# Compressed keys and values of a sparse-attention layer: bank reads shared with ScalarE, entries and key copies placed anew

## The chip, the cores and the metric

The kernel runs on one core of one Trainium2 chip. The metric is the device time of one execution in microseconds. The core's engines are TensorE (PE in the profile, its weight loads PEld), VectorE (DVE), ScalarE (ACT), GpSimd (POOL) and SyncE (SP, which issues the DMAs here). Each runs its own instructions in order, and they wait for each other by semaphores.

## The reference

A two-layer decoder trunk over 512 tokens of width 1024, in float32: layer 0 mixes by mLSTM and differential attention, layer 1 by sparse attention with three branches, and each has a SwiGLU network behind it. The change lies in layer 1's compressed branch. Its keys and values, four groups of 64 features, are cut into 31 blocks of 32 tokens at a distance of 16. A block is flattened and goes through a small network:

```python
def compress_blocks(kv, pos_emb, w1, w2):
    B, S, G, d = kv.shape
    r = CMP_BLOCK // CMP_STRIDE
    n_chunks = S // CMP_STRIDE
    n_cmp = n_chunks - r + 1
    ch = kv.reshape(B, n_chunks, CMP_STRIDE, G, d)
    blocks = jnp.concatenate([ch[:, j:j + n_cmp] for j in range(r)], axis=2)
    blocks = blocks + pos_emb[None, None, :, None, :]
    flat = blocks.transpose(0, 1, 3, 2, 4).reshape(B, n_cmp, G, CMP_BLOCK * d)
    return jax.nn.silu(flat @ w1) @ w2
```

The selected and the window branch have keys with a rotary embedding (KS and KW below); the queries (Q) are rotated as well.

## The kernel before

The weights come as **units**, some 512 KB each, in the order of `UNIT_LIST` (line 93). SP loads unit u into one of four buffers `raw`, once unit u-4 is split (`load`, line 550). Each float32 weight is split into a high part (`split_high`, ScalarE copies it into `w_high`, type fp32r; line 578) and a low part (`split_low`, VectorE subtracts; line 597), two buffers each. So the split of unit u+2 waits until TensorE is through with unit u. TensorE multiplies each tile three times, high by high, low by high and high by low (`mm3`, lines 705 to 707): 24 matmuls of 512 columns for a feature unit.

Layer 1 takes its units in this order: KC 0, KC 1, VC 0, VC 1 (keys and values to be compressed, two groups of 64 features each), KS 0, KS 1, KW 0, C1K 0, KW 1, Q 0, C1K 1, Q 1, C1K 2, Q 2, C1K 3, Q 3, Q 4, C1V 0, Q 5, C1V 1, Q 6, C1V 2, Q 7, GT, C1V 3, then VSW. C1K and C1V are the first weights of the small network. They have 12 matmuls of 256 columns, so the unit behind each of them comes soon, and its split is made in two **halves** (`HALVED`, line 98): the high half may start once TensorE is half through unit u-2 (semaphore `half_read`, ScalarE line 567), the second waits for its end (line 570); VectorE follows at lines 586 and 589.

On ScalarE and on VectorE one loop runs over the units: first the split of unit u+2, then `post(u)`, what is to be done with the result of unit u. Nothing is reordered: what waits in `post(u)` holds back the split of unit u+3.

- For a KC or VC unit VectorE **reads the bank** four times (line 1986), times `rinv`, the reciprocal norm of the tokens: each group of 64 features goes into `k_cmp_dup` or `v_cmp_dup` (`kvd`) twice, in the lower 64 partitions as it is, in the upper 64 moved by one token. The first of them waits for `rinv`, which ScalarE takes from TensorE in its `post(KC 0)` (line 1383).
- 32 **entries**, 16 of keys and 16 of values, are the inputs of C1K and C1V (four entries to a unit). For each, ScalarE adds the position and writes a high part (`cmp_high`, line 1553), and VectorE makes the low part (`cmp_low`, line 2055). `CMP_FIRST` (line 184) says at which unit's `post` which entries are made. TensorE waits for them (`hidden_unit`).
- For KS, KW and Q units VectorE takes the bank (line 1805), shuffles (line 1877) and does the rotary steps (lines 1887, 1888, 1892), with entries between them: the first behind the shuffle, the second behind line 1888, the rest at the end.
- ScalarE makes **key copies** (`duplicate_keys`, line 1532): four copies of 64 rows by 512 for each of KS 0, KS 1, KW 0 and KW 1, in the `post` of the unit that `DUP_AT` names, one place later. VectorE's next use but one of the same work buffer waits for them (`dup_done`).
- The hidden rows of the small network are turned on TensorE (line 1114), the keys' behind Q 3, the values' in VSW 0.

Of the kernel before, what the change touches and what calls it, by code (L numbers as in the profile page):

```python
# [5 lines left out]
ALU = mybir.AluOpType  # L6
# [5 lines left out]
P = 128  # L12
# [128 lines left out]
def plan_banks():  # L141
    bank, used, nxt, turn = {}, [0] * 8, 0, 0
    for kind, k in TILES:
# [22 lines left out]
        else:  # L166
# [14 lines left out]


DUP_AT = [("KS", 1), ("KW", 0), ("KW", 1), ("Q", 0)]
CMP_FIRST = {("VC", 1): 0, ("KS", 0): 1, ("KS", 1): 4, ("KW", 0): 7, ("KW", 1): 10, ("Q", 0): 13, ("Q", 1): 16,
             ("Q", 2): 19, ("Q", 3): 22, ("Q", 4): 25, ("Q", 5): 28, ("Q", 6): 30}


def cmp_entries(unit):
# [175 lines left out]
def trunk(nc, A, consts, out):  # L364
    with ExitStack() as ctx:
# [190 lines left out]

            return w[:, 0:KT * P].rearrange("p (k s g h) -> p k s g h", s=2, g=2, h=32)[:, :, side, :, 0:4]

        def split_high(act, u, it=0, per=0):
            if u >= UNITS:  # L560
                return
            w = width(u)
            act.wait_ge(S(f"raw_in{u % RAW}"), 16 * loads_in_slot(u) + it * (16 * per // RAW))
            if u in HALVED:

                act.wait_ge(S("half_read"), HALVED.index(u) + 1)
                act.activation(wh[u % SPL][:, 0:w // 2], raw[u % RAW][:, 0:w // 2], ACT.Copy)\
                    .then_inc(S("half_high"), 1)
                wait_unit(act, u - SPL)
                act.activation(wh[u % SPL][:, w // 2:w], raw[u % RAW][:, w // 2:w], ACT.Copy)\  # L570
                    .then_inc(S("split_high"), 1)
                return
            if u >= SPL:
                wait_unit(act, u - SPL, it, per)
            dst, src = wh[u % SPL][:, 0:w], raw[u % RAW][:, 0:w]
            if u == FIRST["IF"]:
                dst, src = if_columns(wh[u % SPL], 0), src.rearrange("p (k g h) -> p k g h", g=2, h=4)
            act.activation(dst, src, ACT.Copy).then_inc(S("split_high"), 1)  # L578
# [123 lines left out]
        def _(pe):  # L702
# [406 lines left out]
            def hidden_turn(name):  # L1109

                v = name == "C1V"
                pe.wait_ge(S("hidden_taken"), 1 + v)
                for hc in range(2):
                    mm = pe.transpose(aux[:, 3, hc * P:hc * P + CCOLS],
                                      hrow[0:CCOLS, 256 * v + hc * P:256 * v + (hc + 1) * P], ident[0:CCOLS, 0:CCOLS])
                mm.then_inc(S("hidden_turned"), 1)

            for m in range(2):
# [250 lines left out]
        def _(act):  # L1369
# [70 lines left out]
            def post(u):  # L1440
# [17 lines left out]
                elif name == "VM" and j == 1:  # L1458
                    act.wait_ge(S("lam_sums"), 2)
                    act.activation(lame, lams, ACT.Exp).then_inc(S("lam_exps"), 1)  # L1460
                elif name == "VM" and j == 2:
                    act.wait_ge(S("u_col"), 1)
                    act.activation(em2col, aux[:, 0, 16:32], ACT.Exp, scale=2.0).then_inc(S("exp_negm"), 1)
                    for h in range(3):
                        act.wait_ge(S("negM_rows"), h + 1)
                        act.activation(nmb[:, tcol(h)], aux[:, 1 + h, :], ACT.Copy).then_inc(S("negM_taken"), 1)
                elif name in ("WO0", "WO1"):
                    n = 1 + 2 * int(name[2])
                    wait_taken(act, (name, j))
                    norm_y(n, j)  # L1470
                    if j == 7:
                        split_high(act, u + SPL)
                    square(n, j)
                elif name == "KC" and j == 0:
                    norm_rows(2)
                elif name in ("Q", "KS", "KW", "VC"):
                    if (name, j) == ("Q", 3):
                        act.wait_ge(S("hidden_turned"), 1)
                        act.activation(hid.rearrange("p (k g n) -> p k g n", k=2, n=CPAD)[:, :, :, 0:NCMP],
                                       aux[:, 3, 0:256].rearrange("p (k m) -> p k m", m=P)[:, :, 0:CCOLS]  # L1480
                                       .rearrange("p k (g n) -> p k g n", n=NCMP), ACT.Copy).then_inc(S("hidden_in"), 1)
                    if (name, j) == ("Q", 4):
                        act.wait_ge(S("kc_product"), 1)
                        kc_pairs = kcd.rearrange("p (g n) -> p g n", n=2 * CPAD)
                        for a in range(2):
                            half, other = slice(64 * a, 64 * a + 64), slice(64 - 64 * a, 128 - 64 * a)
                            act.activation(kc_pairs[other, :, col(a, CPAD)],
                                           kc[other, 0:P].rearrange("p (g n) -> p g n", n=CPAD), ACT.Copy, scale=0.0)
                            o = act.activation(kc_pairs[half, :, col(a, CPAD)],
                                               ps(("KCD", 0))[half, 0:P].rearrange("p (g n) -> p g n", n=CPAD), ACT.Copy)  # L1490
                        o.then_inc(bank_free(("KCD", 0)), 1)
                    for e in cmp_entries((name, j)):
                        cmp_high(e)
                    if (name, j) in DUP_AT:
                        duplicate_keys(DUP_AT.index((name, j)))
                elif name in ("C1K", "C1V") and j == 3:
                    wait_unit(act, u)
                    act.activation(hrow[0:CCOLS, col(name == "C1V", 256)], aux[0:CCOLS, 2, 0:256], ACT.Silu)\
                       .then_inc(S("hidden_taken"), 1)
                    if name == "C1V":  # L1500
                        cmp_exp(1)
                elif name == "GT":
                    cmp_exp(0)
                elif name == "VSW":
                    if j == 0:

                        act.wait_ge(S("hidden_turned"), 2)
                        act.wait_ge(S("v_hidden_zero"), 2)
                        for hc in range(2):
                            turned = aux[:, 3, hc * P:hc * P + CCOLS].rearrange("p (g n) -> p g n", n=NCMP)  # L1510
                            act.activation(vhid[hc].rearrange("p (g h n) -> p g h n", h=4, n=CPAD)[:, :, :, 0:NCMP],
                                           turned.unsqueeze(2).to_broadcast([P, GROUPS, 4, NCMP]), ACT.Copy)\
                               .then_inc(S("hidden_in"), 1)
                    if j == 1:
                        act.wait_ge(S("gates_added"), 1)
                        act.activation(gates, gates, ACT.Sigmoid).then_inc(S("gates"), 1)
                    if j == 3:
                        for i in (0, 2):
                            act.wait_ge(S("rows_done"), i + 1)
                            taken_scaled(vsw[:, tcol(i)], (name, i), i)  # L1520
                    cmp_take(j)
                    if j < 2:
                        cmp_exp(j + 2)

            def duplicate_keys(k):

                r = 8 + k
                act.wait_ge(S("rope_done"), 3 * r + 3)
                dst = ksd if k < 2 else kwd
                for g in range(2):  # L1530
                    for half in range(2):
                        o = act.activation(dst[64 * half:64 * half + 64, tcol(2 * (k % 2) + g)],
                                           tmp[r % 2][64 * g:64 * g + 64, 0:T], ACT.Copy)
                o.then_inc(S("dup_done"), 1)

            def cmp_exp(i):
                act.wait_ge(S("c_shifted"), i + 1)
# [8 lines left out]
            def cmp_high(e):  # L1546
                v, c = e // CHUNKS, e % CHUNKS
                if c == 0:
                    wait_taken(act, (("KC", "VC")[v], 0))
                    wait_taken(act, (("KC", "VC")[v], 1))  # L1550
                if v and c % 4 == 0:
                    wait_unit(act, AT["C1K", c // 4])
                act.activation(kph[:, c * CCOLS:(c + 1) * CCOLS].rearrange("p (g n) -> p g n", n=NCMP),
# [153 lines left out]
            ffn(0)  # L1707
            for u in range(FIRST["KC"], FIRST["WO1"]):
                if u < FIRST["WO1"] - 1:
                    split_high(act, u + SPL)  # L1710
                post(u)

            def rows_high(q):
# [63 lines left out]
        def _(dve):  # L1777
# [128 lines left out]
            def post(u):  # L1906
# [68 lines left out]
                elif name in ("KC", "VC"):  # L1975
# [4 lines left out]
                        dve.wait_ge(S("rinv"), 3)  # L1980
                    dst = kvd[name == "VC"]

                    for g in range(2):
                        rows_ = slice(64 * g, 64 * g + 64)
                        for half in range(2):
                            o = dve.tensor_tensor(dst[64 * half:64 * half + 64,
                                                      (2 * j + g) * T:(2 * j + g + 1) * T - half],
                                                  ps((name, j))[rows_, half:T], rinv[rows_, half:T], ALU.mult)
                    o.then_inc(bank_free((name, j)), 1)
                    for e in cmp_entries((name, j)):  # L1990
                        cmp_low(e)
                elif name == "GT":
# [649 lines left out]
```

## Time and profile before

| | us |
|---|---|
| median of 3 runs | 1340.31 (1339.85 to 1340.4) |
| the profiled execution | 1340.15 |
| its span, first to last instruction | 1338.4 |
| TensorE busy | 1319.6 |
| VectorE busy | 698.0 |
| ScalarE busy | 553.1 |

The profile is of one execution. Its page gives the busy time of each engine, the groups of instructions by line, and the chain that ended last, of which TensorE has 89% and VectorE 5%. The mean granted clock of TensorE is 0.999 of its full speed. In the timelines a row is one instruction or a few alike; a wait is put down to the instruction that released it. The matmuls of TensorE overlap in the records (0.39 us each, one every 0.23 us), so their distance from start to start counts.

### The profile page before, as it was taken

The numbers are of one execution on the slowest core, as the hardware profiler recorded it, in microseconds if no ns is written. First come the engines' busy times: TensorE is split into PE (matmuls) and PEld (weight loads), VectorE is DVE, ScalarE is ACT, GpSimd is POOL, SyncE is SP. The second block draws the span as 40 slices with busy tenths as digits, with TensorE's granted clock in tenths as the row PEclk, the third lists the DMA queues.
The fourth block names the chain that finished last, engine by engine and source line by source line (L and its number), as shares of the span: only waits on it lengthen the run. The fifth ranks groups of instructions, "written<-read, shape, count | busy, mean of one in ns | idle before, by whom it ended". The sixth has DMA issues, their size and how long they took to land.

```text
span 1338.4 us, 17983 instructions
## 1 busy us (share of the span) xinstructions
PE 1319.6 (99%) x6420; PEld 1050.8 (79%) x6420; DVE 698.0 (52%) x1282; ACT 553.1 (41%) x1012; POOL 229.8 (17%) x233
## 2 busy tenths in 40 slices
PE   9999999999999999999999999999999999999997
PEld 7677688888888888888878865567888888888887
DVE  5479886544333334332699778775533344332222
ACT  4435665443333332222274457784433333332222
POOL 2047571221111110100000002112211111110100
PEclk9999999999999999999999999999999999999999
DMA  8331222333333333332244310000333333343311
GB/s 239 89 79 49 63 64 66 92 94 95 94 98 103 95 106 108 107 87 78 80 118 124 96 32 1 17 2 17 106 97 96 94 94 94 95 119 106 104 47 64
DMA packets 205481, 114.12 MB, mean 85 GB/s; under 512 B 5712, under 2 KB 202576, under 8 KB 205296
## 3 DMA queue, kind: packets, MB, share of 16 engines
q1 hardware_dynamic: 204800, 112.97, 29.1%
q0 software_dynamic: 416, 0.35, 0.3%
q8 instruction: 33, 0.54, 0.2%
q14 instruction: 24, 0.20, 0.0%
q10 hardware_dynamic: 208, 0.06, 0.0%
HBM read 111.27 MB, written 2.10 MB: 85 GB/s over the span
## 4 chain that ended last, share of the span: by engine, by line
PE 89%; DVE 5%; ACT 2%; issue 2%; POOL 1%; DMA 0%; POOLq 0%; DVEq 0%; SPq 0%; ACTq 0%
PE acc L705 24%; PE acc L707 24%; PE acc L706 24%; PE acc L1285 3%; PE aux L1272 2%; PE aux L1190 2%; PE acc L1190 1%; DVE w_low L597 1%; PE acc L1272 1%; ACT w_high L578 1%; PE acc L1172 1%; PE aux L1151 1%; PE aux L883 0%; PE acc L825 0%; PE aux L893 0%
## 5 line engine op out<-in xcount | busy, mean ns | idle before, releaser
L597 DVE TENSOR_TENSOR w_low<-raw,w_high 128x1024 fp32r<-128x1024 f32 (+2 forms) x185 | 247.5, 1338 | 491.9 <-ACT w_high L578 491.7
L705 PE MATMUL acc<-y_high,w_high 128*128 128x512 f32 x992 | 392.0, 395 | 2.5 <-DVE w_low L589 2.0
L707 PE MATMUL acc<-y_high,w_low 128*128 128x512 f32 x992 | 386.6, 390 | 0.0
L706 PE MATMUL acc<-y_low,w_high 128*128 128x512 f32 x992 | 386.2, 389 | 0.0
L578 ACT ACTIVATE w_high<-raw 128x1024 fp32r<-128x1024 f32 (+2 forms) x186 | 205.7, 1106 | 301.4 <-PE acc L707 296.1
L705 PEld LDWEIGHTS acc<-y_high,w_high 128*128 128x128 f32 x992 | 185.8, 187 | 43.1 <-DVE w_low L589 3.3
L707 PEld LDWEIGHTS acc<-y_high,w_low 128*128 128x128 f32 x992 | 185.7, 187 | 40.0
L706 PEld LDWEIGHTS acc<-y_low,w_high 128*128 128x128 f32 x992 | 185.9, 187 | 38.7 <-issue 0.7
L705 PE MATMUL acc<-ffn_high,w_high 128*128 128x512 f32 (+1 forms) x374 | 141.0, 377 | 0.0
L706 PE MATMUL acc<-ffn_low,w_high 128*128 128x512 f32 (+1 forms) x374 | 140.8, 377 | 0.0
L707 PE MATMUL acc<-ffn_high,w_low 128*128 128x512 f32 (+1 forms) x374 | 140.8, 377 | 0.0
L2513 POOL TENSOR_TENSOR work<-work,work 128x512 f32<-128x512 f32 x44 | 56.9, 1294 | 417.7 <-DVE work L1805 417.7
L1567 ACT ACTIVATE ffn_high<-work 128x512 f32 (+1 forms) x44 | 27.8, 632 | 148.4 <-POOL work L2513 148.4
L1805 DVE TENSOR_TENSOR work<-acc,rinv 128x512 f32<-128x512 f32 x107 | 73.2, 684 | 17.1 <-PE acc L707 9.7
L2499 POOL TENSOR_TENSOR work<-work,work 128x512 f32<-128x512 f32 x31 | 42.1, 1359 | 224.0 <-ACT work L1379 223.5
L705 PEld LDWEIGHTS acc<-ffn_high,w_high 128*128 128x128 f32 x374 | 70.4, 188 | 12.9
L706 PEld LDWEIGHTS acc<-ffn_low,w_high 128*128 128x128 f32 x374 | 70.4, 188 | 12.9
L707 PEld LDWEIGHTS acc<-ffn_high,w_low 128*128 128x128 f32 x374 | 70.4, 188 | 12.8
L1732 ACT ACTIVATE score<-score,neg_max 128x384 f32<-128x384 f32 (+3 forms) x128 | 68.6, 540 | 14.1 <-DVE neg_max L2378 14.1
L2605 POOL TENSOR_TENSOR o_rows<-o_rows,work 128x512 f32<-128x512 f32 x16 | 20.4, 1273 | 249.7 <-DVE work L2400 249.7
L1562 ACT ACTIVATE work<-work 128x512 f32<-128x512 f32 x44 | 27.8, 632 | 80.3 <-DVE work L1805 80.3
L1372 ACT ACTIVATE y_high<-residual,feature_params 128x512 fp32r<-128x512 f32 x32 | 22.8, 722 | 51.5 <-DVE residual L2005 33.0
(342 smaller groups left out, 1685.8 us busy)
## 6 DMA issues: line engine op xcount, KB each, us to landing
raw<-in_l_w_in_dram SPq DMA_DIRECT2D x44, 512.0 KB, 3.8
raw<-in_l_w_gate_dram SPq DMA_DIRECT2D x44, 512.0 KB, 3.8
raw<-in_l_w_up_dram SPq DMA_DIRECT2D x44, 512.0 KB, 3.8
raw<-in_l_w_down_dram SPq DMA_DIRECT2D x32, 704.0 KB, 4.5
raw<-in_l_w_out_dram SPq DMA_DIRECT2D x16, 512.0 KB, 3.5
x_rows<-in_x_dram SPq DMA_DIRECT2D x4, 512.0 KB, 7.6
raw<-in_l_cmp_w_k_dram SPq DMA_DIRECT2D x4, 512.0 KB, 3.7
raw<-in_l_cmp_w_v_dram SPq DMA_DIRECT2D x4, 512.0 KB, 3.7
```

The costliest lines, as they stand in the source:

```text
L578: act.activation(dst, src, ACT.Copy).then_inc(S("split_high"), 1)
L597: dve.tensor_tensor(dst, src, high.bitcast(F32), ALU.subtract).then_inc(S("split_low"), 1)
L705: pe.matmul(o, ah, bh, start=first, stop=False)
L706: pe.matmul(o, ah, bl, start=False, stop=False)
L707: return pe.matmul(o, al, bh, start=False, stop=last)
L1190: pe.matmul(scores_at(n), qrot[a, q], k, start=True, stop=True).then_inc(S("s_scores"), 1)
L1272: mm = pe.transpose(turn_bank(("probs", t))[:, c + s * P:c + (s + 1) * P], probs[:, col(s)], ident)
L1285: mm = pe.matmul(ps(("OB", b))[64 * g:64 * g + 64, :].rearrange("p (h q) -> p h q", q=P), vsw[:, v:v + HD], probs[:, 4 * g:4 * g + 4, col(s)],
L1732: act.activation(probs_at(n), probs_at(n), ACT.Exp, scale=-1.0, bias=nmx[:, n % 16:n % 16 + 1], accum_out=rsum[:, n % 16:n % 16 + 1]).then ...
L1805: return dve.tensor_tensor(dst, ps(tile)[lo:hi, cols], rinv[lo:hi, cols], ALU.mult)
L2499: pool.tensor_tensor(tmp[0][:, 0:T], tmp[0][:, 0:T], tmp[1 + m % 2][:, 0:T], ALU.add)\
L2513: pool.tensor_tensor(up, tmp[2 * (t % 2)][:, 0:T], up, ALU.mult).then_inc(S("ffn_prod"), 1)
```

## The change

Four edits, all in layer 1's compressed branch and the keys beside it.

1. For a KC or VC unit VectorE reads the bank twice instead of four times, plus one column: the even group into the lower partitions, the odd group, moved by one token, into the upper ones. ScalarE makes the other halves from these (`move_tokens`, two copies of 64 rows by 511) in its `post` of the same unit, behind VectorE's reads. `cmp_high` waits for these copies (`tokens_moved`) instead of the reads.
2. Entries: three at VC 0, three at VC 1, one at KS 0, one at KS 1, two at KW 0, one at KW 1, then three a unit from Q 0 to Q 6. Before: one at VC 1, then three a unit, with two at Q 5 and Q 6.
3. Of the key copies of KS 0 and KW 0 the first two stay where they were; the third goes between the two high halves of the split of KW 1 and Q 1, the fourth behind the second half.
4. The hidden rows are activated and turned with 128 rows instead of 124.

```diff
--- before.py
+++ after.py
@@ -181,8 +181,9 @@
 
 
 DUP_AT = [("KS", 1), ("KW", 0), ("KW", 1), ("Q", 0)]
-CMP_FIRST = {("VC", 1): 0, ("KS", 0): 1, ("KS", 1): 4, ("KW", 0): 7, ("KW", 1): 10, ("Q", 0): 13, ("Q", 1): 16,
-             ("Q", 2): 19, ("Q", 3): 22, ("Q", 4): 25, ("Q", 5): 28, ("Q", 6): 30}
+COPIES_LATE = {("KW", 1): 0, ("Q", 1): 2}
+CMP_FIRST = {("VC", 0): 0, ("VC", 1): 3, ("KS", 0): 6, ("KS", 1): 7, ("KW", 0): 8, ("KW", 1): 10, ("Q", 0): 11,
+             ("Q", 1): 14, ("Q", 2): 17, ("Q", 3): 20, ("Q", 4): 23, ("Q", 5): 26, ("Q", 6): 29}
 
 
 def cmp_entries(unit):
@@ -556,7 +557,7 @@
 
             return w[:, 0:KT * P].rearrange("p (k s g h) -> p k s g h", s=2, g=2, h=32)[:, :, side, :, 0:4]
 
-        def split_high(act, u, it=0, per=0):
+        def split_high(act, u, it=0, per=0, after_half=None):
             if u >= UNITS:
                 return
             w = width(u)
@@ -566,6 +567,8 @@
                 act.wait_ge(S("half_read"), HALVED.index(u) + 1)
                 act.activation(wh[u % SPL][:, 0:w // 2], raw[u % RAW][:, 0:w // 2], ACT.Copy)\
                     .then_inc(S("half_high"), 1)
+                if after_half:
+                    after_half()
                 wait_unit(act, u - SPL)
                 act.activation(wh[u % SPL][:, w // 2:w], raw[u % RAW][:, w // 2:w], ACT.Copy)\
                     .then_inc(S("split_high"), 1)
@@ -1111,8 +1114,7 @@
                 v = name == "C1V"
                 pe.wait_ge(S("hidden_taken"), 1 + v)
                 for hc in range(2):
-                    mm = pe.transpose(aux[:, 3, hc * P:hc * P + CCOLS],
-                                      hrow[0:CCOLS, 256 * v + hc * P:256 * v + (hc + 1) * P], ident[0:CCOLS, 0:CCOLS])
+                    mm = pe.transpose(aux[:, 3, col(hc)], hrow[:, 256 * v + hc * P:256 * v + (hc + 1) * P], ident)
                 mm.then_inc(S("hidden_turned"), 1)
 
             for m in range(2):
@@ -1471,9 +1473,11 @@
                     if j == 7:
                         split_high(act, u + SPL)
                     square(n, j)
-                elif name == "KC" and j == 0:
-                    norm_rows(2)
-                elif name in ("Q", "KS", "KW", "VC"):
+                elif name in ("Q", "KS", "KW", "KC", "VC"):
+                    if (name, j) == ("KC", 0):
+                        norm_rows(2)
+                    if name in ("KC", "VC"):
+                        move_tokens(name, j)
                     if (name, j) == ("Q", 3):
                         act.wait_ge(S("hidden_turned"), 1)
                         act.activation(hid.rearrange("p (k g n) -> p k g n", k=2, n=CPAD)[:, :, :, 0:NCMP],
@@ -1495,7 +1499,7 @@
                         duplicate_keys(DUP_AT.index((name, j)))
                 elif name in ("C1K", "C1V") and j == 3:
                     wait_unit(act, u)
-                    act.activation(hrow[0:CCOLS, col(name == "C1V", 256)], aux[0:CCOLS, 2, 0:256], ACT.Silu)\
+                    act.activation(hrow[:, col(name == "C1V", 256)], aux[:, 2, 0:256], ACT.Silu)\
                        .then_inc(S("hidden_taken"), 1)
                     if name == "C1V":
                         cmp_exp(1)
@@ -1522,16 +1526,30 @@
                     if j < 2:
                         cmp_exp(j + 2)
 
+            def move_tokens(name, j):
+
+                dst = kvd[name == "VC"]
+                first, second = 2 * j * T, (2 * j + 1) * T
+                wait_taken(act, (name, j))
+                act.activation(dst[64:128, first:first + T - 1], dst[0:64, first + 1:first + T], ACT.Copy)\
+                   .then_inc(S("tokens_moved"), 1)
+                act.activation(dst[0:64, second + 1:second + T], dst[64:128, second:second + T - 1], ACT.Copy)\
+                   .then_inc(S("tokens_moved"), 1)
+
+            def duplicate_part(k, part):
+
+                r, g, half = 8 + k, part // 2, part % 2
+                if part == 0:
+                    act.wait_ge(S("rope_done"), 3 * r + 3)
+                o = act.activation((ksd if k < 2 else kwd)[64 * half:64 * half + 64, tcol(2 * (k % 2) + g)],
+                                   tmp[r % 2][64 * g:64 * g + 64, 0:T], ACT.Copy)
+                if part == 3:
+                    o.then_inc(S("dup_done"), 1)
+
             def duplicate_keys(k):
 
-                r = 8 + k
-                act.wait_ge(S("rope_done"), 3 * r + 3)
-                dst = ksd if k < 2 else kwd
-                for g in range(2):
-                    for half in range(2):
-                        o = act.activation(dst[64 * half:64 * half + 64, tcol(2 * (k % 2) + g)],
-                                           tmp[r % 2][64 * g:64 * g + 64, 0:T], ACT.Copy)
-                o.then_inc(S("dup_done"), 1)
+                for part in range(2 if k in COPIES_LATE.values() else 4):
+                    duplicate_part(k, part)
 
             def cmp_exp(i):
                 act.wait_ge(S("c_shifted"), i + 1)
@@ -1546,8 +1564,7 @@
             def cmp_high(e):
                 v, c = e // CHUNKS, e % CHUNKS
                 if c == 0:
-                    wait_taken(act, (("KC", "VC")[v], 0))
-                    wait_taken(act, (("KC", "VC")[v], 1))
+                    act.wait_ge(S("tokens_moved"), 4 + 4 * v)
                 if v and c % 4 == 0:
                     wait_unit(act, AT["C1K", c // 4])
                 act.activation(kph[:, c * CCOLS:(c + 1) * CCOLS].rearrange("p (g n) -> p g n", n=NCMP),
@@ -1707,7 +1724,10 @@
             ffn(0)
             for u in range(FIRST["KC"], FIRST["WO1"]):
                 if u < FIRST["WO1"] - 1:
-                    split_high(act, u + SPL)
+                    late = COPIES_LATE.get(stage_of(u + SPL))
+                    split_high(act, u + SPL, after_half=None if late is None else lambda k=late: duplicate_part(k, 2))
+                    if late is not None:
+                        duplicate_part(late, 3)
                 post(u)
 
             def rows_high(q):
@@ -1980,13 +2000,12 @@
                         dve.wait_ge(S("rinv"), 3)
                     dst = kvd[name == "VC"]
 
-                    for g in range(2):
-                        rows_ = slice(64 * g, 64 * g + 64)
-                        for half in range(2):
-                            o = dve.tensor_tensor(dst[64 * half:64 * half + 64,
-                                                      (2 * j + g) * T:(2 * j + g + 1) * T - half],
-                                                  ps((name, j))[rows_, half:T], rinv[rows_, half:T], ALU.mult)
-                    o.then_inc(bank_free((name, j)), 1)
+                    first, second = 2 * j * T, (2 * j + 1) * T
+                    low, high = slice(0, 64), slice(64, 128)
+                    dve.tensor_tensor(dst[low, first:first + T], ps((name, j))[low, :], rinv[low, :], ALU.mult)
+                    dve.tensor_tensor(dst[low, second:second + 1], ps((name, j))[high, 0:1], rinv[high, 0:1], ALU.mult)
+                    dve.tensor_tensor(dst[high, second:second + T - 1], ps((name, j))[high, 1:T], rinv[high, 1:T],
+                                      ALU.mult).then_inc(bank_free((name, j)), 1)
                     for e in cmp_entries((name, j)):
                         cmp_low(e)
                 elif name == "GT":
```

## Rows read from the trace of the kernel before

**Rows 1.** The page, part 1: busy us, share of the span, instructions.
```profile
PE 1319.6 (99%) x6420; PEld 1050.8 (79%) x6420; DVE 698.0 (52%) x1282; ACT 553.1 (41%) x1012; POOL 229.8 (17%) x233
```

**Rows 2.** Waits of TensorE, 640 to 800 us: total, times, longest.
```profile
PE acc L705 <- DVE w_low L589: 2.0, 2, 1.0
```

**Rows 3.** Timeline of TensorE: start us, us, instruction, idle before and releaser.
```profile
655.08 0.39 PE L705 MATMUL acc<-y_high,w_high 128*128 128x512 f32 x1
...
660.52 0.39 PE L705 MATMUL acc<-y_high,w_high 128*128 128x512 f32 x1
...
679.41 0.50 PE L705 MATMUL acc<-y_high,w_high 128*128 128x512 f32 x1 [1.00 <-DVE w_low L589]
...
684.98 0.39 PE L705 MATMUL acc<-y_high,w_high 128*128 128x512 f32 x1
...
693.00 0.50 PE L705 MATMUL acc<-y_high,w_high 128*128 128x512 f32 x1 [0.99 <-DVE w_low L589]
...
713.71 0.50 PE L705 MATMUL acc<-y_high,w_high 128*128 128x512 f32 x1 [0.38 <-DVE w_low L597]
```

**Rows 4.** Timeline of ScalarE, 640 to 742 us.
```profile
650.28 1.05 ACT L578 ACTIVATE w_high<-raw 128x1024 fp32r<-128x1024 f32 x1
...
677.04 0.63 ACT L570 ACTIVATE w_high<-raw 128x512 fp32r<-128x512 f32 x1
677.58 1.30 ACT L1553 ACTIVATE cmp_in_high<-k_cmp_dup,feature_params 128x124 fp32r<-128x124 f32 x3
678.78 2.54 ACT L1532 ACTIVATE k_sel_dup<-work 64x512 f32<-64x512 f32 x4
```

**Rows 5.** Timeline of VectorE, 640 to 755 us.
```profile
650.42 2.79 DVE L1986 TENSOR_TENSOR k_cmp_dup<-acc,rinv 64x512 f32<-64x512 f32 x4 [4.07 <-ACT rinv L1383]
653.25 1.23 DVE L597 TENSOR_TENSOR w_low<-raw,w_high 128x1024 fp32r<-128x1024 f32 x1
654.50 2.79 DVE L1986 TENSOR_TENSOR k_cmp_dup<-acc,rinv 64x512 f32<-64x512 f32 x4
...
668.57 0.69 DVE L1805 TENSOR_TENSOR work<-acc,rinv 128x512 f32<-128x512 f32 x1
...
670.25 0.69 DVE L1887 TENSOR_TENSOR work<-work,shape_constants 128x512 f32<-128x512 f32 x1
670.85 0.69 DVE L1888 TENSOR_TENSOR work<-work,shape_constants 128x512 f32<-128x512 f32 x1
...
672.75 1.22 DVE L597 TENSOR_TENSOR w_low<-raw,w_high 128x1024 fp32r<-128x1024 f32 x1
673.90 0.68 DVE L1805 TENSOR_TENSOR work<-acc,rinv 128x512 f32<-128x512 f32 x1
...
678.08 0.67 DVE L586 TENSOR_TENSOR w_low<-raw,w_high 128x512 fp32r<-128x512 f32 x1
678.68 0.68 DVE L589 TENSOR_TENSOR w_low<-raw,w_high 128x512 fp32r<-128x512 f32 x1
...
742.37 1.23 DVE L597 TENSOR_TENSOR w_low<-raw,w_high 128x1024 fp32r<-128x1024 f32 x1 [2.69 <-ACT w_high L578]
743.51 0.68 DVE L1805 TENSOR_TENSOR q_raw<-acc,rinv 128x512 f32<-128x512 f32 x1
...
745.01 0.69 DVE L1887 TENSOR_TENSOR work<-q_raw,shape_constants 128x512 f32<-128x512 f32 x1
...
746.34 0.69 DVE L1892 TENSOR_TENSOR q_rot<-work,work 128x512 f32<-128x512 f32 x1
```

**Rows 6.** Groups of VectorE by form: count, busy us, mean ns, idle before.
```profile
L2378 DVE DVE_READ_ACCUMULATOR2_ANT neg_max<- 128x1 f32 x128 | 10.6, 83 | 0.0
...
L1794 DVE TENSOR_SCALAR msq<-aux 128x4 f32<-128x4 f32 x3 | 0.5, 155 | 0.0
```

**Rows 7.** Groups of TensorE by line, same columns.
```profile
L1114 PE MATMUL aux<-shape_constants,hidden_rows 124*128 124x124 f32 x4 | 0.8, 282 | 0.0
```

## The prediction

> **What bounds the kernel now.** I read the page's busy shares first: TensorE is busy for 99% of the span, the next engine, VectorE, for 52% [rows 1]. So only what makes TensorE wait, or gives it other work, can move the end. The waits of TensorE come next, cut to the stretch of the compressed keys and values (640 to 800 us): two waits of 1.0 us for the second low half of a weight split on VectorE [rows 2]. TensorE's timeline places them in front of KW 1 (679.41) and Q 1 (693.00), shows one of 0.38 us in front of Q 4 (713.71), and gives the beat: 5.44 us from one unit to the next, 5.57 us behind a unit that began late [rows 3]. A stall that is taken away anywhere is gained whole, and one that is added is paid whole, since nothing later waits.
>
> Who is late there? Read ScalarE's and VectorE's timelines side by side. In front of KW 1 ScalarE's second half of the split starts at 677.04, as soon as KW 0 is multiplied, and ends at 677.67 [rows 4]; VectorE, busy with the rotary steps of KS 1 and its entries, starts the first low half at 678.08 and the second at 678.68, which ends at 679.36 [rows 5]. So at both waits of 1.0 us VectorE's queue is the last, not ScalarE's. With VectorE free, KW 1 could start about 0.9 us sooner (677.67 + 0.03 + 0.68 + 0.05 = 678.43).
>
> **Part 1, half of the bank reads become ScalarE copies.** Now a KC or VC unit costs VectorE four reads, 2.79 us, 0.70 apart [rows 5]. After the change: a read of 64 rows by 512 (0.70), one column, a read of 64 by 511 (0.69). No row shows a read of one column. The nearest is the bank read of 128 by 4 at 0.155 us; from below there is the accumulator read of 0.083 [rows 6], from above a whole read of 0.69, which gets little weight, as the durations of VectorE go by columns (0.155 for 4, 0.69 for 512, 1.23 for 1024). I take 0.16, so a T (the reads of one unit) is 1.55 us. ScalarE gets a move M of two copies of 64 by 511: four key copies of 64 by 512 take 2.54 us [rows 4], so M = 1.27 us. Does VectorE's saving count? Only if nothing new waits, and M is a wait: it is queued in front of the next ScalarE split.
>
> The order on ScalarE is: split of unit u+2 (SH, 1.06), then M of unit u, which waits for T of unit u, then entries; on VectorE: low split of u+2 (SL, 1.23, which waits for SH), then T of unit u, 1.25 behind SL's start [rows 5]. Before the change nothing of ScalarE waited for T in this stretch, and SH of VC 1 ran at 650.28, ahead of the reads. Now the two engines form one ring. Handovers are 0.03 (ScalarE to VectorE), 0.04 (VectorE to ScalarE) and 0.05 us (VectorE to TensorE), from ends and starts in the timelines [rows 3 to 5]. I walk it from the first read, 650.42, which waits for rinv as before:
>
> T of KC 0 ends 651.97; M 652.01 to 653.28; SH of VC 1 to 654.34; SL 654.37 to 655.60. TensorE wanted VC 1 at 655.08 [rows 3] and gets it at 655.65: 0.57 late.
> T of KC 1 655.62 to 657.17; M to 658.48; SH of KS 0 to 659.54; SL 659.57 to 660.80. KS 0 is wanted at 655.65 + 5.57 = 661.22: in time.
> T of VC 0 to 662.37; M to 663.68; the three entries that now sit here, 0.40 each (three in 1.30, the next instruction 1.20 behind the first [rows 4]), to 664.89; SH of KS 1 to 665.95; SL 665.98 to 667.21. Wanted at 666.66, there at 667.26: 0.60 late.
> T of VC 1 from 667.23 to 668.78; M to 670.09; three entries to 671.30; SH of KW 0 to 672.36; SL 672.39 to 673.62; KW 0 starts 673.67, wanted at 667.26 + 5.57 = 672.83: 0.84 late.
>
> The ring takes 5.20 us a unit without entries, less than TensorE's 5.44, and 6.41 with three: it holds for VC 0 and VC 1, where the change puts entries.
>
> The Trainium skill, VectorE: DVE Perf Modes, section "Two Vector instructions with no wait between them", says that a Vector instruction whose input or output starts in another group of 32 partitions than the last one's waits until that has finished. The bank reads stand 0.70 apart and two rotary steps on all rows 0.60 (670.25 and 670.85) [rows 5], so the rows agree, and the three new reads, which change halves as well, keep the 0.70. Had they run unheld, the four T would be 0.1 to 0.2 shorter each and the sum below 0.4 to 0.8 us less.
>
> **Part 2, entries sooner.** KS 0, KS 1 and KW 1 keep one entry of three, KW 0 two of three. On VectorE the block behind a take lasts 4.18 us with three entries (668.57 to 672.75) and 4.18 again (673.90 to 678.08) [rows 5]. Q 7 has none: 743.51 to its last add at 746.34, plus 0.60, is 3.43 [rows 5]; an entry behind the shuffle fills a wait there and is estimated at 0.18 (take to first rotary step 1.68 at KS 0, 1.50 at Q 7). So a block with one entry is 3.61, 0.57 less (bounds 0.56 and 0.70, the second if no wait is laid bare).
> VectorE's block for KS 0 now starts at 672.39 + 1.25 = 673.64 instead of 668.57: 5.07 later. From there to KW 1's second low half VectorE never waits for ScalarE (its first and second halves are there by 678.6 and 680.2). Two blocks save 2 x 0.57. KW 1 starts at 679.41 + 5.07 - 1.14 = 683.34, **3.93 us late**. Between KW 1 and Q 1 TensorE sets the pace again: the split of C1K 1 waits for the end of KW 1, so that the block of KW 1 begins 3.93 late too and is 0.57 shorter. Q 1 starts 3.36 late, and its old wait of 1.0 us has become some 0.4.
> KW 0 with two entries (about 3.82) ends before the split of Q 0 is wanted: VectorE through with it at 688.26, TensorE wants it at 688.91. Cover: 0.65 us.
>
> **Part 3, key copies around the halves.** Four copies stay four copies; one goes between the halves of the split and one behind. ScalarE's second half was already in time [rows 4], so taking the copies from in front buys nothing. The third copy lies in ScalarE's wait for TensorE, the fourth (0.64) delays the next entries, which have over 1 us to spare, and the read of KW 0, which waits for the copies: those end 0.64 us behind the second half, while VectorE then still works on the low half (0.68). Nothing; at worst 0.1 us each at KW 1 and at C1K 2. Without that cover it is 0.64.
>
> **Part 4, turns of 128 rows.** Two transposes for the keys and two for the values, 282 ns each at 124 rows [rows 7], now 128 by 128. Q 4 behind the first pair waits for VectorE [rows 3]; the second pair ends up to 0.02 us later. Nothing. The activations go by columns, also unchanged. Behind Q 1 the entries stay three a unit up to Q 6 (one more at Q 5 and at Q 6, 0.35 us of VectorE each, under its waits for ScalarE; the one behind Q 6 is 2.69 us [rows 5]). Loads are issued behind the low split of the unit four places ahead and land in some 4 us by the page: covered. The wait in front of Q 4 stays.
>
> **Sum.** 5.07 - 1.14 - 0.57 = +3.36 us on the profiled execution's 1340.15 us: 1343.5. The median of the runs shown is 1340.31, 0.16 above it; I forecast **1343.6**.
>
> **Rivals.**
> *The reads are cheaper than I set them.* The column costs 0.08 and the reads follow at 0.60: T = 1.37, four of them save 0.72: +2.6 us, 1342.9. For it: no row has these reads in this order. Against: the old reads, which change halves as well, are all 0.70 apart. Chance 0.17.
> *The ring never closes (the other side, not slower).* Place: ScalarE's queue between rinv and the split of KW 0. If T, M, three entries, SH and SL together took under 5.44 us instead of 6.41, TensorE would stay ahead, and only the shorter blocks would count: 0.57 at KW 1 and 0.57 at Q 1, -1.1 us, 1339.1. It decides from 1.0 us less a unit, as would copies of 0.15 us; the four copies of this shape take 0.63 each [rows 4]. Chance 0.07. Even all three waits gone would be -2.4 us plus restarts, so a gain of over 0.2% is nearly excluded.
> *The clock.* The wait in front of KW 1 grows from 1.0 to 2.7 us. Through today's waits the granted clock stays 1.00; no row shows a longer one here. If the lower level (1.2 of 2.4 GHz) held for one unit behind it, 5.4 us more: 1349. Chance 0.03.
> The Trainium skill, TensorE: Matmul & The Clock Gate, Part 1, says that idleness lowers the clock; no run here shows whether this wait does.
> *The cuts do nothing and the ring is longer* (a column read costs a full 0.69, or the copies wait on each other): 4 x 0.5 more, +5.5 us, 1345.8. Chance 0.08.
>
> **How the numbers follow.** Forecast (+3.0 to +3.9) 0.65, the rivals as above. 0.2% of 1340 is 2.7 us, about what a measurement of this kernel can tell from no change. The forecast's own band lies over it, the first rival just around it. Slower by over 0.2%: 0.65 x 0.95 + 0.17 x 0.4 + 0.03 + 0.08 = 0.79, lowered to 0.72 for what I may have overlooked in the queues; same 0.25; faster 0.03. The range goes from 1341.8 (below the first rival, with 0.8 for errors of many small terms) to 1345.3.
>
> **What the profile after would show.** VC 1, KS 1 and KW 0 each start behind a wait of 0.5 to 0.9 us for a VectorE low split whose releaser is ScalarE; ScalarE idles for VectorE's reads before each move; the wait in front of KW 1 is 2.5 to 2.8 us, that of Q 1 about 0.4, that of Q 4 as now. VectorE is less busy and waits more. I am wrong if SH of VC 1 starts before 652.5, if KW 0 starts on the beat, or if KW 1 waits under 1 us.

## The result, and the profile after

The changed kernel takes 1345.29 us (median of 9 runs, 1343.67 to 1345.57) against 1340.03 (9 runs): 1.0035 of before, 95% interval 1.0026 to 1.0043. The forecast was 1343.6, with 1341.8 to 1345.3. The nine runs lie in two groups, three at 1343.67 to 1344.02 and six at 1345.20 to 1345.57; what parts them is the subject of one experiment (busy wait). The median lies 0.01 us inside the forecast's upper end, three of the nine runs lie above it.

The page says little: TensorE is 1.7 us busier and its span 5.2 us longer than in [rows 1], 1343.6 us.

```profile
PE 1321.3 (98%) x6420; PEld 1050.8 (78%) x6420; DVE 693.5 (52%) x1278; ACT 558.1 (42%) x1020; POOL 229.7 (17%) x233
```

The waits of TensorE from 640 to 800 us, total, times and longest. In the changed kernel the matmuls of a unit stand in lines 708 to 710, the low splits in 600 (whole), 589 and 592 (halves). These answer to [rows 2].

```profile
PE acc L708 <- DVE w_low L592: 3.0, 2, 2.5
PE acc L708 <- DVE w_low L600: 2.1, 4, 0.7
```

Where before there were two waits of 1.0 us for a second half, there is one of 2.5 us and one of 0.4, and four for a whole split (three of them new). TensorE's timeline has them all (start, duration, instruction, idle before), as [rows 3] had them of before:

```profile
655.34 0.50 PE L708 MATMUL acc<-y_high,w_high 128*128 128x512 f32 x1 [0.46 <-DVE w_low L600]
...
667.05 0.50 PE L708 MATMUL acc<-y_high,w_high 128*128 128x512 f32 x1 [0.52 <-DVE w_low L600]
...
673.52 0.50 PE L708 MATMUL acc<-y_high,w_high 128*128 128x512 f32 x1 [0.71 <-DVE w_low L600]
...
683.21 0.50 PE L708 MATMUL acc<-y_high,w_high 128*128 128x512 f32 x1 [2.55 <-DVE w_low L592]
...
684.50 0.56 PE L710 MATMUL acc<-y_high,w_low 128*128 128x512 f32 x1
...
685.28 0.63 PE L709 MATMUL acc<-y_low,w_high 128*128 128x512 f32 x1
685.70 0.63 PE L710 MATMUL acc<-y_high,w_low 128*128 128x512 f32 x1
...
688.13 0.39 PE L710 MATMUL acc<-y_high,w_low 128*128 128x512 f32 x1
...
697.89 0.50 PE L708 MATMUL acc<-y_high,w_high 128*128 128x512 f32 x1 [0.43 <-DVE w_low L592]
...
718.61 0.50 PE L708 MATMUL acc<-y_high,w_high 128*128 128x512 f32 x1 [0.36 <-DVE w_low L600]
```

In order: VC 1, KS 1, KW 0, KW 1 (683.21, behind 2.55 us), four matmuls inside KW 1, Q 1 and Q 4. ScalarE's timeline shows what the new waits are made of. Lines 1534 and 1536 are the moves, 581 a split, 1570 the entries; compare with [rows 4], where the split of VC 1 ran at 650.28, right behind `rinv`.

```profile
649.43 0.60 ACT L1385 ACTIVATE rinv<-aux 128x512 f32<-128x512 f32 x1 [6.60 <-PE aux L799]
651.66 0.63 ACT L1534 ACTIVATE k_cmp_dup<-k_cmp_dup 64x511 f32<-64x511 f32 x1 [1.63 <-DVE k_cmp_dup L2007]
652.31 0.63 ACT L1536 ACTIVATE k_cmp_dup<-k_cmp_dup 64x511 f32<-64x511 f32 x1
652.97 1.06 ACT L581 ACTIVATE w_high<-raw 128x1024 fp32r<-128x1024 f32 x1
656.91 0.63 ACT L1534 ACTIVATE k_cmp_dup<-k_cmp_dup 64x511 f32<-64x511 f32 x1 [2.88 <-DVE k_cmp_dup L2007]
...
662.17 0.63 ACT L1534 ACTIVATE v_cmp_dup<-v_cmp_dup 64x511 f32<-64x511 f32 x1 [2.89 <-DVE v_cmp_dup L2007]
...
663.48 1.31 ACT L1570 ACTIVATE cmp_in_high<-k_cmp_dup,feature_params 128x124 fp32r<-128x124 f32 x3
664.70 1.04 ACT L581 ACTIVATE w_high<-raw 128x1024 fp32r<-128x1024 f32 x1
...
679.18 0.63 ACT L1544 ACTIVATE k_sel_dup<-work 64x512 f32<-64x512 f32 x1
679.83 0.63 ACT L573 ACTIVATE w_high<-raw 128x512 fp32r<-128x512 f32 x1
```

The move at 651.66 idled 1.63 us for VectorE's reads, and the split of VC 1 had to stand behind it until 652.97. It is the same again at 656.91 and 662.17, with 2.9 us of idling each, and for VC 1 at 668.63. On VectorE (the three reads are lines 2005 to 2007, the take of KS 0 is at 673.50; compare [rows 5]) the low split of VC 1 waits for that split in turn:

```profile
650.06 0.68 DVE L2005 TENSOR_TENSOR k_cmp_dup<-acc,rinv 64x512 f32<-64x512 f32 x1 [4.07 <-ACT rinv L1385]
650.76 0.16 DVE L2006 TENSOR_TENSOR k_cmp_dup<-acc,rinv 64x1 f32<-64x1 f32 x1
650.93 0.69 DVE L2007 TENSOR_TENSOR k_cmp_dup<-acc,rinv 64x511 f32<-64x511 f32 x1
654.06 1.23 DVE L600 TENSOR_TENSOR w_low<-raw,w_high 128x1024 fp32r<-128x1024 f32 x1 [2.44 <-ACT w_high L581]
...
672.24 1.23 DVE L600 TENSOR_TENSOR w_low<-raw,w_high 128x1024 fp32r<-128x1024 f32 x1 [0.52 <-ACT w_high L581]
673.50 0.69 DVE L1825 TENSOR_TENSOR work<-acc,rinv 128x512 f32<-128x512 f32 x1
...
677.12 1.22 DVE L600 TENSOR_TENSOR w_low<-raw,w_high 128x1024 fp32r<-128x1024 f32 x1
...
681.87 0.68 DVE L589 TENSOR_TENSOR w_low<-raw,w_high 128x512 fp32r<-128x512 f32 x1
682.47 0.68 DVE L592 TENSOR_TENSOR w_low<-raw,w_high 128x512 fp32r<-128x512 f32 x1
```

The engine that was to be relieved idles for 2.44 us instead. Executions differ by up to 1 us in what lies before this stretch (the first read starts at 650.42 in the trace of before and 650.06 here), so places are counted below from the start of the first read of each trace. In the trace of before KS 1 and KW 0 start at 665.96 and 671.40.

| start, us behind the first read | before | foretold | measured after |
|---|---|---|---|
| VC 1 | 4.66 | 5.23 | 5.28 |
| KS 1 | 15.54 | 16.84 | 16.99 |
| KW 0 | 20.98 | 23.25 | 23.46 |
| KW 1 | 28.99 | 32.92 | 33.15 |
| Q 1 | 42.58 | 45.94 | 47.83 |

Up to KW 1 the foretold places are 0.05 to 0.23 us short. From KW 1 to Q 1 something else came in: 1.66 us more than foretold. The windows of the trace (busy time and count of each engine, then the granted clock and the DMAs) show it:

```profile
core 0: us, PE busy (x) PEld busy (x) DVE busy (x) ACT busy (x) POOL busy (x), PEclk, DMA share, GB/s
683.00:684.00 1.00, 0.79 (x3) 0.67 (x4) 0.96 (x4) 0.98 (x3) 0.00 (x0) 1.00 0.00 0
684.00:685.00 1.00, 1.00 (x5) 0.78 (x4) 1.00 (x3) 0.97 (x2) 0.00 (x0) 0.78 0.52 99
685.00:687.00 2.00, 2.00 (x7) 1.52 (x6) 2.00 (x5) 0.62 (x1) 0.00 (x0) 0.50 0.60 213
687.00:688.00 1.00, 1.00 (x4) 0.81 (x3) 1.00 (x1) 0.00 (x0) 0.00 (x0) 0.51 0.00 0
688.00:692.00 4.00, 4.00 (x19) 3.29 (x18) 0.33 (x2) 1.31 (x2) 0.00 (x0) 1.00 0.49 131
```

The granted clock is 0.50 from about 684.5 to 688, the level of 1.2 GHz, and the matmuls are 0.42 us apart there (685.28 and 685.70 above) instead of 0.23. That begins 1.3 us behind the end of the wait of 2.55 us. The nine matmuls from 684.50 to 688.13 take 3.63 us instead of 9 x 0.227 = 2.04: 1.6 us.

### The profile page after: what moved, and what is told of

The parts are those of the page before. It is cut to its first block, busy times and chain, and to the rows that moved or that the text cites. A ratio compares the mean times of both kernels' runs of the same rounds, so it can differ in the third digit from the quotient of the medians.

```text
span 1343.6 us, 17986 instructions
## 1 busy us (share of the span) xinstructions
PE 1321.3 (98%) x6420; PEld 1050.8 (78%) x6420; DVE 693.5 (52%) x1278; ACT 558.1 (42%) x1020; POOL 229.7 (17%) x233
## 4 chain that ended last, share of the span: by engine, by line
PE 87%; DVE 6%; ACT 3%; issue 2%; POOL 1%; DMA 0%; SPq 0%; POOLq 0%; DVEq 0%; ACTq 0%
PE acc L708 24%; PE acc L710 23%; PE acc L709 23%; PE acc L1287 3%; PE aux L1274 2%; PE aux L1192 2%; DVE w_low L600 1%; PE acc L1192 1%; ACT w_high L581 1%; PE acc L1274 1%; PE acc L1174 1%; PE aux L1153 1%; PE aux L886 0%; PE acc L828 0%; DVE step L2201 0%
```

## The experiments

All but small parts are edits of the changed kernel, and all were timed in rounds beside the kernel before, whose medians were 1340.12 (first four) and 1340.22 (last two).

**Four reads.** The first part of the change is undone, the rest stays.

```diff
-                    if name in ("KC", "VC"):
-                        move_tokens(name, j)
...
-                    dve.tensor_tensor(dst[low, first:first + T], ps((name, j))[low, :], rinv[low, :], ALU.mult)
...
+                    for g in range(2):
+                        rows_ = slice(64 * g, 64 * g + 64)
+                        for half in range(2):
```

> The changed kernel with the four bank reads on VectorE again and no copies on ScalarE; entries, key copies and turns as changed. Theory (the ring of VectorE's reads and ScalarE's copies delays the next split): the ring is open, ScalarE's split of VC 1 runs ahead of the reads again, VC 1, KS 1 and KW 0 start on the beat, and only the shorter blocks behind KS 1 and KW 1 count: 0.57 us each, -1.1 us against before, 1338.9. Rival (the new places of the entries cost the time): still +3 us or more, 1343. Rival (nothing is gained by shorter blocks, the waits go back to 1.0 us): 1340.0.

Measured: 1338.97 us (11 runs, 1338.75 to 1339.37), 0.9991 of before (0.9982 to 1.0000). ScalarE's timeline has its splits at 650.14, 655.19 and 660.63, each as TensorE releases it, and TensorE keeps the two waits for second halves only, at 0.45 and 0.42 us:

```profile
650.14 1.05 ACT L581 ACTIVATE w_high<-raw 128x1024 fp32r<-128x1024 f32 x1
655.19 1.06 ACT L581 ACTIVATE w_high<-raw 128x1024 fp32r<-128x1024 f32 x1 [4.00 <-PE acc L710]
657.24 1.33 ACT L1569 ACTIVATE cmp_in_high<-k_cmp_dup,feature_params 128x124 fp32r<-128x124 f32 x3 [0.99 <-DVE k_cmp_dup L2005]
660.63 1.06 ACT L581 ACTIVATE w_high<-raw 128x1024 fp32r<-128x1024 f32 x1 [2.06 <-PE acc L710]
```

```profile
678.70 0.50 PE L708 MATMUL acc<-y_high,w_high 128*128 128x512 f32 x1 [0.45 <-DVE w_low L592]
...
691.75 0.50 PE L708 MATMUL acc<-y_high,w_high 128*128 128x512 f32 x1 [0.42 <-DVE w_low L592]
```

KW 1 lies 28.43 us behind the first read (0.56 sooner than before) and Q 1 41.48 (1.10 sooner), as foretold for the shorter blocks (0.57 and 1.14). So the places of the entries and key copies aren't what costs, and the loss comes from the first part. This is also the fastest kernel of the study, 1.15 us below the kernel before. Its interval just reaches no change, but all eleven runs lie below the lowest of the 23 of before (1339.76).

**Late moves.** Does the first part cost by its copies or by where they stand? Here every instruction is kept and each move waits in the queue one unit longer.

```diff
-                    if name in ("KC", "VC"):
-                        move_tokens(name, j)
+                    late_move = {("KC", 1): ("KC", 0), ("VC", 0): ("KC", 1), ("VC", 1): ("VC", 0),
+                                 ("KS", 0): ("VC", 1)}.get((name, j))
+                    if late_move:
+                        move_tokens(*late_move)
```

> The changed kernel with every instruction kept, but ScalarE's copies of a unit's tokens made one unit later, so that they wait for reads that are long done. Theory (it is the order in ScalarE's queue that costs): as with four reads, -1.1 us, 1338.9, and no wait in front of VC 1, KS 1 and KW 0. Rival (the copies themselves, 10 us of ScalarE in all with what they wait for, cost the time wherever they stand): still +3 us, 1343.

Measured: 1339.25 us (11 runs, 1339.00 to 1342.05), 0.9996 (0.9987 to 1.0005). ScalarE's timeline: the split of VC 1 (650.93) now runs ahead of the moves of KC 0, and that of KS 0 (655.98) waits for TensorE again.

```profile
650.93 1.05 ACT L581 ACTIVATE w_high<-raw 128x1024 fp32r<-128x1024 f32 x1
652.66 0.63 ACT L1536 ACTIVATE k_cmp_dup<-k_cmp_dup 64x511 f32<-64x511 f32 x1 [0.69 <-DVE k_cmp_dup L2009]
...
655.98 1.06 ACT L581 ACTIVATE w_high<-raw 128x1024 fp32r<-128x1024 f32 x1 [2.03 <-PE acc L710]
```

KW 1 starts 28.43 and Q 1 41.46 us behind the first read, the same as with four reads to 0.02 us; the median is 0.3 us above that kernel's, of which this stretch shows nothing (in the profiled execution 0.8 us lie ahead of the first read, which starts at 651.07 instead of 650.27). In this stretch the ScalarE copies cost nothing; their place in front of the next split cost it all. What the 0.3 us are is not shown. Halving VectorE's reads brings nothing beyond that, for VectorE was not late in this stretch.

**Old entries.** The moves stay, the entries go back.

```diff
-CMP_FIRST = {("VC", 0): 0, ("VC", 1): 3, ("KS", 0): 6, ("KS", 1): 7, ("KW", 0): 8, ("KW", 1): 10, ("Q", 0): 11,
-             ("Q", 1): 14, ("Q", 2): 17, ("Q", 3): 20, ("Q", 4): 23, ("Q", 5): 26, ("Q", 6): 29}
+CMP_FIRST = {("VC", 1): 0, ("KS", 0): 1, ("KS", 1): 4, ("KW", 0): 7, ("KW", 1): 10, ("Q", 0): 13, ("Q", 1): 16,
+             ("Q", 2): 19, ("Q", 3): 22, ("Q", 4): 25, ("Q", 5): 28, ("Q", 6): 30}
```

> The changed kernel with the entries at the units of before (one at VC 1, three at each of KS 0 to Q 4, two at Q 5 and Q 6). Theory (ring): without entries a turn of the ring is 5.25 us, under TensorE's 5.44, so KS 1 and KW 0 start on the beat and only VC 1 is 0.5 us late. But VectorE's block of KS 0 still stands behind the low split of KW 0, which ends near 671.6 instead of 668.5, and its two blocks are 0.57 longer than in the changed kernel: KW 1 starts 3.1 us later than before, behind a wait of about 3.6 us, and nothing is won back at Q 1: 1343.1 at full clock, 1344.8 if the granted clock falls behind that wait. Rival (the entries that the change puts into the ring are what costs): +0.6 us, 1340.6.

Measured: 1345.29 us (5 runs, 1344.84 to 1346.31), 1.0039 (1.0025 to 1.0052). TensorE's timeline at KW 1 and Q 1:

```profile
682.30 0.79 PE L708 MATMUL acc<-y_high,w_high 128*128 128x512 f32 x1 [3.49 <-DVE w_low L592]
...
698.43 0.50 PE L708 MATMUL acc<-y_high,w_high 128*128 128x512 f32 x1 [0.99 <-DVE w_low L592]
```

The wait in front of KW 1 is 3.49 us, KW 1 starts 32.22 us behind the first read (+3.23 against before), and no other unit but VC 1 waits before it. So the entries are not what makes the ring costly. Without them TensorE keeps its beat through KS 1 and KW 0, and still pays 3.2 us at KW 1: VectorE's take of KS 0 stands behind the low split of KW 0, 21.42 us behind the first read instead of 18.15.

The granted clock falls here as well, and sooner: TensorE does nothing from 680 to 682, in the middle of the wait, and the clock is already low for a part of it.

```profile
core 0: us, PE busy (x) PEld busy (x) DVE busy (x) ACT busy (x) POOL busy (x), PEclk, DMA share, GB/s
680.00:682.00 2.00, 0.00 (x0) 0.00 (x0) 2.00 (x5) 1.88 (x4) 0.00 (x0) 0.73 0.03 9
683.00:690.00 7.00, 7.00 (x23) 5.53 (x22) 4.54 (x8) 1.36 (x2) 0.00 (x0) 0.66 0.41 119
```

From KW 1 to Q 1 it is 16.13 us, where the kernel before, with the same wait of 0.99 in front of Q 1, takes 13.59: the clock costs 2.5 us here instead of 1.6. That is why the median is 0.5 us above the 1344.8 expected with a fall of the clock, and no lower than that of the changed kernel, although KW 1 starts 0.9 us sooner.

**Busy wait.** TensorE gets work of no use in the long wait, nothing else changes.

```diff
             hidden_unit("C1K", 0)
+            for _ in range(8):
+                pe.matmul(aux[:, 3, :], yh[:, 0:P], yh[:, 0:T], start=True, stop=True)
             feature_unit(AT["KW", 1], ("KW", 1))
```

> The changed kernel with eight more matmuls of 128 by 512 (0.23 us apart, 1.8 us in all, their result unused) on TensorE in the wait in front of KW 1, which is 2.55 us in the changed kernel's profile. Theory (the idle time lets the granted clock fall for 3.4 us, which costs 1.7 us, in most executions): the clock stays at 1.00, KW 1 starts at the same time, and all executions are near 1343.7, +3.7 us. Rival (the two groups of times have another source): a median near 1345.3, or two groups again; if the added matmuls reach into the split, a few tenths more.

Measured: 1343.89 us (7 runs, 1343.66 to 1344.30), 1.0027 (1.0016 to 1.0039). The windows and the starts of KW 1 and Q 1:

```profile
core 0: us, PE busy (x) PEld busy (x) DVE busy (x) ACT busy (x) POOL busy (x), PEclk, DMA share, GB/s
680.00:683.00 3.00, 2.58 (x15) 1.89 (x13) 2.96 (x6) 2.94 (x6) 0.00 (x0) 1.00 0.54 153
...
684.00:688.00 4.00, 4.00 (x20) 3.25 (x19) 4.00 (x7) 1.66 (x2) 0.00 (x0) 1.00 0.46 131
```

```profile
683.27 0.50 PE L708 MATMUL acc<-y_high,w_high 128*128 128x512 f32 x1 [0.69 <-DVE w_low L592]
...
696.34 0.50 PE L708 MATMUL acc<-y_high,w_high 128*128 128x512 f32 x1 [0.43 <-DVE w_low L592]
```

The clock stays at 1.00. KW 1 starts 33.15 us behind the first read, exactly as in the changed kernel, Q 1 46.22 instead of 47.83: 1.61 us sooner. All seven runs lie within 0.3 us of the changed kernel's three lower ones, none near its six upper ones. Doing more work on TensorE makes the kernel 1.4 us faster (the two were timed in different rounds, with the kernel before at 1340.03 and 1340.12). That the two groups are executions in which the clock falls and in which it doesn't follows from these times. The mean granted clocks on record agree: 0.998 in all three lower runs, 0.997 in five of the six upper ones and 0.998 in the sixth, where 3.4 us at half the clock would make 0.0013 of 1343.6 us. Of the lower ones themselves no trace was taken, so it isn't shown directly.

**Small parts.** The kernel before with parts 3 and 4 alone (reads and entries as before).

```diff
+COPIES_LATE = {("KW", 1): 0, ("Q", 1): 2}
...
-                act.wait_ge(S("rope_done"), 3 * r + 3)
...
+                for part in range(2 if k in COPIES_LATE.values() else 4):
+                    duplicate_part(k, part)
...
-                    split_high(act, u + SPL)
+                    late = COPIES_LATE.get(stage_of(u + SPL))
+                    split_high(act, u + SPL, after_half=None if late is None else lambda k=late: duplicate_part(k, 2))
+                    if late is not None:
+                        duplicate_part(late, 3)
...
+                    mm = pe.transpose(aux[:, 3, col(hc)], hrow[:, 256 * v + hc * P:256 * v + (hc + 1) * P], ident)
```

> The kernel before with only the two small edits: the third and fourth key copy around the halves of the split, and the hidden rows activated and turned with 128 rows. Theory: nothing, within 0.2 us of before, 1340.1, both waits of 1.0 us as they were, since ScalarE's second half was in time already. Rival (the copies kept ScalarE's halves late): -0.5 to -1.2 us, 1339.2.

Measured: 1340.31 us (11 runs, 1339.97 to 1341.67), 1.0002 (0.9993 to 1.0011). The waits for second halves are the old ones:

```profile
PE acc L708 <- DVE w_low L592: 2.0, 2, 1.0
```

KW 1 lies 28.99 us behind the first read, as before. Nothing gained, nothing lost.

**No entries.** Four reads, and no entry at all in the blocks in front of the two waits.

```diff
-CMP_FIRST = {("VC", 0): 0, ("VC", 1): 3, ("KS", 0): 6, ("KS", 1): 7, ("KW", 0): 8, ("KW", 1): 10, ("Q", 0): 11,
+CMP_FIRST = {("VC", 0): 0, ("VC", 1): 3, ("KS", 0): 6, ("KW", 0): 8, ("Q", 0): 11,
```

> The kernel with four reads on VectorE, and the entries moved further: three at VC 0 and at VC 1, two at KS 0, none at KS 1, three at KW 0, none at KW 1, three from Q 0 on. Theory (VectorE's block is what TensorE waits for in front of KW 1 and Q 1): each block is 0.75 us shorter than before, 4.18 to 3.43, -1.5 us, 1338.6, with waits of 0.25 us left. Rival (another handover takes over once the entries are gone): as with one entry, -1.1 us, 1338.9.

Measured: 1339.41 us (11 runs, 1338.94 to 1340.26), 0.9994 (0.9985 to 1.0003). TensorE's timeline at KW 1 and C1K 2:

```profile
679.31 0.50 PE L708 MATMUL acc<-y_high,w_high 128*128 128x512 f32 x1 [0.27 <-DVE w_low L592]
...
698.42 0.38 PE L708 MATMUL aux<-w_high,cmp_in_high 128*124 128x256 f32 x1 [0.34 <-DVE w_low L600]
```

The wait in front of KW 1 is down to 0.27 us and that of Q 1 is gone, but C1K 2 now waits 0.34 us: its split stands on ScalarE behind three entries and the four key copies of KW 1, which can't start before Q 1's second half. Q 4 lies 62.27 us behind the first read, with four reads 62.21. The rival is right: one entry is as good as none, and the next handover has taken over. In ScalarE's queue ahead of those entries also stands the fourth copy of KW 0, which part 3 of the change put behind the second half (691.60, 0.65 us to the next instruction). Whether C1K 2 would wait without it was not tested; small parts shows part 3 as free only while VectorE is the later engine.

## Why the prediction was right or wrong

- **The range**: it holds by luck. The forecast of 1343.6 is 1.7 us short, and its upper end of 1345.3 lies 0.01 us above the median, though no term of it stood for what made up the difference, the clock (below). The three lower runs, 1343.67 to 1344.02, are what the forecast's sum describes.
- **The ring** (the forecast's mechanism): right. All three new waits stand where the steps put them, with the releasers named. T took 1.56 us (1.55 foretold; the one column 0.16), M 1.31 instead of 1.27, since a move lets the next instruction start 0.65 behind it, not 0.635. Four moves make that 0.16 of the 0.23 us by which KW 1 was late against the forecast. Four reads and late moves, in which the ring is open and the whole loss is gone, show that it is this ring.
- **The blocks**: right. 3.62 us for KS 0 (673.50 to 677.12), 3.61 foretold. Four reads gains 1.10 us by them, 1.14 foretold.
- **The entries' part in the ring**: the sentence that the ring fits TensorE's beat without them is right (old entries: KS 1 and KW 0 on the beat), but it could be read as if entries made the loss, and they don't. Without them VectorE's take of KS 0 comes 3.27 us later than before (18.15 to 21.42), with them 5.29 (23.44; the forecast had 5.07). So they add 2.0 us there, and give back 1.1 by the two shorter blocks in front of KW 1 (9.71 us from that take to KW 1 instead of 10.80) and 0.56 by the third (Q 1 waits 0.43 instead of 0.99).
- **Key copies and turns of 128 rows**: right, nothing (small parts). The third copy (679.18) went in front of the second half, which started at 679.83; VectorE didn't come to the split before 681.87. That the fourth copy has cover at C1K 2 holds for this kernel; in no entries it stands in the queue that C1K 2 waits for.
- **The clock**: the step that failed. It stood among the rivals with a chance of 0.03 and a price of 5.4 us, a whole unit at half the clock. Measured: by their times in six of nine runs, and 1.6 us, for the low clock ended in the middle of the unit. The sum without it, 5.07 - 1.14 - 0.57 = 3.36, answers to busy wait's 3.64 us at Q 1 and 3.8 us in the medians; with it the changed kernel stands at 5.25 at Q 1 and 5.26 in the medians. The wait was right to 0.15 us (2.7 foretold, 2.55 measured); what would follow it was left out of the sum, as no row of before had a wait longer than 1.2 us.
- **The rule of held instructions** (the Trainium skill, VectorE: DVE Perf Modes, section "Two Vector instructions with no wait between them"), by which a read that starts in another partition group than the last waits for its end: the new trace agrees. The reads stand 0.70 and 0.17 us apart, none starts before the one ahead has ended.

## What to carry to other kernels

Before work is moved to a less busy engine, look at what is queued behind it there. A step that waits for the other engine, put in front of a step for which that engine waits, ties both into one ring, and busy shares of 52% and 41% do not help. The same copies one place later in the queue cost nothing. And a wait of TensorE has a second price beside its length, if the clock falls in it or behind it: 1.6 and 2.5 us in two traces here.

## What the runs showed of the hardware

The granted clock of TensorE fell to its lower level (0.50) 1.3 us behind the end of a wait of 2.55 us, in a profiled execution whose engine was 98% busy, and came back about 3.4 us later, at a cost of 1.6 us. In old entries it fell within the wait of 3.49 us, at a cost of 2.5 us behind it. The waits of 1.0 us before and in small parts, and that of 0.7 us left in busy wait, had no such effect; no trace here has a wait of TensorE between 1.3 and 2.55 us. The Trainium skill, TensorE: Matmul & The Clock Gate, Part 1, says that the clock is lowered by default and released by activity, and that the moment of its rise at the start of a kernel varies from run to run. Both falls behind idleness agree with the first. That the moment of a fall varies too would fit the two groups of times, but no run here shows it.

A VectorE read of one column out of a bank takes 0.16 us where one of 512 takes 0.68, and keeps the next one waiting for its full length.
